# Gate and up of an expert pair issued expert by expert, with per-slot loads, an earlier lower-half scatter for the last pair and later LayerNorm parameter loads

## What is computed

```python
def moe(x, router_w, router_bias, w_gate, w_up, w_down, sw_gate, sw_up, sw_down):
    ...
    def expert_block(args):
        b_tok, b_w, e = args
        xb = xt[b_tok]
        h = jax.nn.silu(xb @ w_gate[e]) * (xb @ w_up[e])
        return (h @ w_down[e]) * b_w[:, None].astype(xt.dtype)
    ...
    routed = jax.ops.segment_sum(y_rows.reshape(rows, d), row_tok, num_segments=t)
    shared = (jax.nn.silu(xt @ sw_gate) * (xt @ sw_up)) @ sw_down
    return (routed + shared).reshape(bsz, s, d)
```

## Time and profile before

| | us |
|---|---|
| runs (three) | 1239.41, 1241.08, 1244.82; median 1241.08 |
| the profiled execution, its own time | 1241.98 |
| its span | 1240.2 |
| TensorE busy in it | 1183.7 (95%) |
| gate and up of both layers, L1216, busy | 226.8 + 118.6 + 115.3 |
| down projection, L1272 from `ew`, busy | 218.4 |

### The profile page before, as it was taken

One profiled execution on the slowest core, in us unless ns is written; L12 is line 12 of the kernel. 1 busy time (PEld: TensorE's weight loads), 2 busy tenths in 40 slices (PEclk: granted clock), 3 DMA queues, 4 the chain that ended last, 5 costly groups with the idle time before them and its releaser, 6 DMA issues.

```text
span 1240.2 us, 17629 instructions
## 1 busy us (share of the span) xinstructions
PE 1183.7 (95%) x7261; PEld 546.2 (44%) x7261; DVE 489.9 (40%) x1059; ACT 193.6 (16%) x330; POOL 47.2 (4%) x78
## 2 busy tenths in 40 slices
PE   9999999999999999988899999999999999998886
PEld 8774833333333333332386757333333333333322
DVE  5895733332323332322237157333333232332224
ACT  3231311111111111110122313111111111111102
POOL 6300100000000000000010001000000000000000
PEclk9999999999999999999989999999999999999998
DMA  9788799999999999999953596999999999999995
GB/s 348 211 300 360 297 383 412 414 422 420 421 421 422 421 421 421 421 421 420 402 190 126 202 382 248 392 414 407 421 421 420 420 422 420 422 421 421 420 420 215
DMA packets 83642, 463.98 MB, mean 374 GB/s; under 512 B 9264, under 2 KB 10608, under 8 KB 38384
## 3 DMA queue, kind: packets, MB, share of 16 engines
q1 hardware_dynamic: 83424, 462.37, 92.2%
q10 hardware_dynamic: 144, 0.52, 0.1%
HBM read 456.51 MB, written 6.36 MB: 373 GB/s over the span
## 4 chain that ended last, share of the span: by engine, by line
PE 72%; DMA 22%; DVE 2%; SPq 1%; ACT 1%; issue 1%; DVEq 0%; POOL 0%; POOLq 0%
PE bank L1216 30%; DMA expert_weights<-in_exp_w_up 21%; PE bank L1272 12%; PE bank L724 5%; PE bank L738 4%; PE bank L1136 4%; PE bank L1166 3%; PE bank L812 2%; PE bank L1154 2%; DMA weight_ring<-in_sh_w_up 1%; PE bank L839 1%; PE bank L1085 1%; PE bank L828 1%; PE bank L1159 1%; PE bank L1232 1%; SPq L316 1%
## 5 line engine op out<-in xcount | busy, mean ns | idle before, releaser
L1216 PE MATMUL bank<-expert_weights,weight_ring 128*64 128x512 f32 x1024 | 226.8, 595 | 12.3 <-DMA expert_weights<-in_exp_w_up 12.3
L1272 PE MATMUL bank<-expert_weights,hiddenT 128*32 128x512 f32 x1888 | 218.4, 595 | 7.8 <-DVE hiddenT L2097 3.6
L2094 DVE TENSOR_TENSOR hidden<-silu_gate,bank 128x256 f32<-128x256 f32 x64 | 26.9, 421 | 391.7 <-ACT silu_gate L1492 391.7
L1216 PEld LDWEIGHTS bank<-expert_weights,weight_ring 128*64 128x64 f32 x1024 | 70.6, 137 | 166.6 <-issue 139.7
L1216 PE MATMUL bank<-expert_weights,hT 128*64 128x512 f32 x512 | 118.6, 606 | 17.2 <-DMA expert_weights<-in_exp_w_up 17.2
L1272 PEld LDWEIGHTS bank<-expert_weights,hiddenT 128*32 128x32 f32 x1888 | 56.4, 109 | 159.3 <-issue 138.9
L1216 PE MATMUL bank<-expert_weights,octet_high 128*64 128x512 f32 x512 | 115.3, 592 | 0.0
L2106 DVE TENSOR_SCALAR y_top<-bank,slot_gate 128x512 fp32r<-128x512 f32 x64 | 48.0, 750 | 126.2 <-PE bank L1272 126.2
L1492 ACT ACTIVATE silu_gate<-bank 128x256 f32<-128x256 f32 x64 | 24.7, 386 | 438.4 <-PE bank L1216 438.4
L1496 ACT ACTIVATE y_top<-bank,slot_gate 128x512 fp32r<-128x512 f32 x64 | 44.0, 687 | 286.4 <-PE bank L1272 286.4
L1216 PEld LDWEIGHTS bank<-expert_weights,hT 128*64 128x64 f32 x512 | 34.3, 138 | 101.4 <-issue 64.5
(11 more groups left out here) (388 smaller groups left out, 1114.2 us busy)
## 6 DMA issues: line engine op xcount, KB each, us to landing
expert_weights<-in_exp_w_down SPq DMA_DIRECT2D x114, 1024.0 KB, 17.2
expert_weights<-in_exp_w_gate SPq DMA_DIRECT2D x108, 1024.0 KB, 14.2
expert_weights<-in_exp_w_up SPq DMA_DIRECT2D x108, 1024.0 KB, 16.3
expert_weights<-in_exp_w_gate SPq DMA_DIRECT2D x40, 512.0 KB, 9.1
expert_weights<-in_exp_w_up SPq DMA_DIRECT2D x40, 512.0 KB, 10.9
weight_ring<-in_w_in_even SPq DMA_DIRECT2D x5, 2048.0 KB, 11.6
spare_down<-in_exp_w_down SPq DMA_DIRECT2D x10, 1024.0 KB, 11.8
weight_ring<-in_w_out SPq DMA_DIRECT2D x4, 2048.0 KB, 7.8
```

The lines of the kernel that those rows point to most:

```text
L1216: last_mm = nc.tensor.matmul(bank[6][a * 2 * CAP:(a + 1) * 2 * CAP, :].rearrange("p (w f) -> p w f", w=2), octet_tokens(l, v, c)[:, 2 * q ...
L1272: last_mm = nc.tensor.matmul(bank[b][by_tile:by_tile + CAP, :], hm[:, j, own:own + CAP], down[a][:, j, half * 512:(half + 1) * 512], start ...
L2094: nc.vector.tensor_tensor(hslot[:, :], sg[:, :], bank[6][:, DE:2 * DE], ALU.mult)\
```

## The change

1. Gate and up of a pair are issued expert by expert: the loop over `a` is now outside the loop over the chunks `c`. TensorE waits for each expert's loads by itself (`gu_in` has one semaphore per slot), and the end of the first expert increments a new semaphore, `gu_first`.
2. SP reloads the first expert's slot after `gu_first` and the second's after `gu_full`. The loads by chunk halves (`expert_chunks`, `BY_HALVES`, `gu_part`, `second_part`, `last_part`) are gone; every gate and up load is of 1 MB.
3. `scatter_last` waits for the lower half's parts (`y_lo`, which `y_low` of columns 0 to 511 now increments too) and adds the lower column half of both tiles, then waits for `y_parts` and adds the upper half.
4. SP waits for the last pair's `gu_full` before it loads LayerNorm's parameters.

```diff
@@ -204,11 +204,9 @@
                   "bt ct stored c_in b_in direct gla_ln gla_last decays masked hstat hstd yhead states y_s5 "
                   "gelu5 out_full")
         for l in range(2):
-            for name in ("gu_in", "d_in"):
-                MO[l][name] = [sem(f"moe{l}_{name}{u}") for u in range(2)]
-            MO[l]["second_part"] = sem(f"moe{l}_second_part")
-            MO[l]["last_part"] = sem(f"moe{l}_last_part")
-            MO[l]["gu_part"] = sem(f"moe{l}_gu_part")
+            MO[l]["gu_in"] = [sem(f"moe{l}_gu_in{s}") for s in range(NSLOT)]
+            MO[l]["d_in"] = [sem(f"moe{l}_d_in{u}") for u in range(2)]
+            MO[l]["gu_first"] = sem(f"moe{l}_gu_first")
             MO[l]["spare_in"] = sem(f"moe{l}_spare_in")
         ring_in = [sem(f"ring_in{i}") for i in range(2)]
 
@@ -313,16 +311,8 @@
         def expert_load(sp, m, l, e, s):
             src_g = A["exp_w_gate"][l, e].rearrange("(p c) f -> p (c f)", c=KC)
             src_u = A["exp_w_up"][l, e].rearrange("(p c) f -> p (c f)", c=KC)
-            sp.dma_start(ew[:, s, 0:EW], src_g).then_inc(m["gu_in"][s // 2], 16)
-            sp.dma_start(ew[:, s, EW:2 * EW], src_u).then_inc(m["gu_in"][s // 2], 16)
-
-        def expert_chunks(sp, l, e, s, chunks, landed):
-
-            lo, hi = chunks[0] * DE, (chunks[-1] + 1) * DE
-            src_g = A["exp_w_gate"][l, e].rearrange("(p c) f -> p (c f)", c=KC)
-            src_u = A["exp_w_up"][l, e].rearrange("(p c) f -> p (c f)", c=KC)
-            sp.dma_start(ew[:, s, lo:hi], src_g[:, lo:hi]).then_inc(landed, 16)
-            sp.dma_start(ew[:, s, EW + lo:EW + hi], src_u[:, lo:hi]).then_inc(landed, 16)
+            sp.dma_start(ew[:, s, 0:EW], src_g).then_inc(m["gu_in"][s], 16)
+            sp.dma_start(ew[:, s, EW:2 * EW], src_u).then_inc(m["gu_in"][s], 16)
 
         def down_half(sp, l, e, s, part, landed):
 
@@ -410,7 +400,6 @@
         def spare_load(sp, m, a, src):
             sp.dma_start(spare_d[a][:, :, :].rearrange("p j n -> p (j n)"), src).then_inc(m["spare_in"], 16)
 
-        BY_HALVES = (2, 3, 4, 5)
         LATE_SLOTS = ((2, 3), (3,))
         LN_INPUT = {"mix0": M0["out_full"], "mix1": M1["out_full"], "moe0": MO[0]["acc_full"], "moe1": MO[1]["acc_full"]}
         LAST_PARTS = ((0, 0, D), (1, 0, 512), (1, 512, D))
@@ -437,57 +426,53 @@
             spare_load(sp, m, 1, down_src(l, 5))
             sp.dma_start(ew[:, 3, 2 * EW:3 * EW], down_src(l, 7)).then_inc(m["d_in"][1], 16)
 
-            def refill(base, it, u, down=None):
-
-                sp.wait_ge(m["gu_full"], (base - 1) * 2 + u + 1)
-                for s in (2 * u, 2 * u + 1):
+            def refill_gu(base, it, u):
+
+                for s, read in ((2 * u, "gu_first"), (2 * u + 1, "gu_full")):
+                    sp.wait_ge(m[read], (base - 1) * 2 + u + 1)
                     expert_load(sp, m, l, it * NSLOT + s, s)
+
+            def refill_d(base, u, experts):
+
                 sp.wait_ge(m["y_hi_full"], (base - 1) * 2 + u + 1)
-                for s in (2 * u, 2 * u + 1):
-                    e = down[s - 2 * u] if down else it * NSLOT + s
+                for s, e in experts:
                     sp.dma_start(ew[:, s, 2 * EW:3 * EW], down_src(l, e)).then_inc(m["d_in"][u], 16)
 
-            def early_refill(ps, pair):
-
-                u = pair % 2
-                first = 2 * pair - 2 * u
-                later = m["last_part" if u else "second_part"]
-                if pair in BY_HALVES:
-                    sp.wait_ge(m["gu_part"], len(BY_HALVES) * ps + BY_HALVES.index(pair) + 1)
-                    for s in (2 * u, 2 * u + 1):
-                        expert_chunks(sp, l, first + s, s, range(0, 4), m["gu_in"][u])
-                sp.wait_ge(m["gu_full"], ps * PAIRS + pair - 1)
-                for s in (2 * u, 2 * u + 1):
-                    if pair in BY_HALVES:
-                        expert_chunks(sp, l, first + s, s, range(4, KC), later)
-                    else:
-                        expert_load(sp, m, l, first + s, s)
-                if pair == 6:
-                    return
-                sp.wait_ge(m["y_hi_full"], ps * PAIRS + pair - 1)
-                if pair == 4:
-                    for a in range(2):
-                        spare_load(sp, m, a, down_src(l, 12 + a))
-                    return
-                for s in (2,) if pair == 3 else (2 * u, 2 * u + 1):
-                    e = first + s + (NSLOT if pair == 2 else 0)
-                    sp.dma_start(ew[:, s, 2 * EW:3 * EW], down_src(l, e)).then_inc(m["d_in"][u], 16)
+            def refill(base, it, u):
+
+                refill_gu(base, it, u)
+                refill_d(base, u, [(s, it * NSLOT + s) for s in (2 * u, 2 * u + 1)])
+
+            def early_refills(ps):
+
+                base = ps * (NE // NSLOT) + 1
+                refill_gu(base, 1, 0)
+                refill_d(base, 0, ((0, 8), (1, 9)))
+                refill_gu(base, 1, 1)
+                refill_d(base, 1, ((2, 6),))
+                base = ps * (NE // NSLOT) + 2
+                refill_gu(base, 2, 0)
+                sp.wait_ge(m["y_hi_full"], (base - 1) * 2 + 1)
+                for a in range(2):
+                    spare_load(sp, m, a, down_src(l, 12 + a))
+                refill_gu(base, 2, 1)
+                refill_d(base, 1, ((2, 10), (3, 11)))
+                base = ps * (NE // NSLOT) + 3
+                refill_gu(base, 3, 0)
+                refill(base, 3, 1)
 
             def last_refill(ps):
 
-                sp.wait_ge(m["gu_full"], ps * PAIRS + PAIRS - 2)
-                for chunks, landed in ((range(0, 4), m["gu_in"][1]), (range(4, KC), m["last_part"])):
-                    for s in (2, 3):
-                        expert_chunks(sp, l, NE - NSLOT + s, s, chunks, landed)
-                sp.wait_ge(m["y_hi_full"], ps * PAIRS + PAIRS - 2)
+                base = ps * (NE // NSLOT) + NE // NSLOT - 1
+                refill_gu(base, NE // NSLOT - 1, 1)
+                sp.wait_ge(m["y_hi_full"], (base - 1) * 2 + 2)
                 for part, landed in enumerate((m["d_in"][1], m["spare_in"])):
                     for s in (2, 3):
                         down_half(sp, l, NE - NSLOT + s, s, part, landed)
 
             def refills(ps):
 
-                for pair in range(2, OCT):
-                    early_refill(ps, pair)
+                early_refills(ps)
                 with sp.Fori(OCT // 2, NE // NSLOT - 1) as it:
                     for u in range(2):
                         refill(ps * (NE // NSLOT) + it, it, u)
@@ -500,11 +485,13 @@
             with sp.If(npass > 1):
                 with sp.Fori(1, npass) as ps:
                     refill(ps * (NE // NSLOT), 0, 0)
-                    refill(ps * (NE // NSLOT), 0, 1, down=(2, 7))
+                    refill_gu(ps * (NE // NSLOT), 0, 1)
+                    refill_d(ps * (NE // NSLOT), 1, ((2, 2), (3, 7)))
                     spare_load(sp, m, 2, down_src(l, 3))
                     for a in range(2):
                         spare_load(sp, m, a, down_src(l, 4 + a))
                     refills(ps)
+            sp.wait_ge(m["gu_full"], npass * PAIRS)
             sp_ln_params(sp, k, A["ln2_w"][l], A["ln2_b"][l])
             return npass
 
@@ -1139,14 +1126,19 @@
 
             def scatter_last(par):
 
+                def add(t, n):
+                    for part in (y_top, y_low):
+                        last = nc.tensor.matmul(bank[2 * t + n][:, :], onehotT[slot_rows(t), par, :],
+                                                part[slot_rows(t), n * 512:(n + 1) * 512], start=False,
+                                                stop=(part is y_low), skip_group_check=True)
+                    return last
+
+                pe.wait_ge(m["y_lo"], npass * (2 * PAIRS))
+                add(0, 0).then_inc(m["acc_full"], 1)
+                add(1, 0)
                 pe.wait_ge(m["y_parts"], npass * PAIRS + 1)
-                for t in range(TT):
-                    for n in range(2):
-                        for part in (y_top, y_low):
-                            last = nc.tensor.matmul(bank[2 * t + n][:, :], onehotT[slot_rows(t), par, :],
-                                                    part[slot_rows(t), n * 512:(n + 1) * 512], start=False,
-                                                    stop=(part is y_low), skip_group_check=True)
-                        last.then_inc(m["acc_full"], 1)
+                add(0, 1).then_inc(m["acc_full"], 1)
+                add(1, 1).then_inc(m["acc_full"], 2)
 
             def add_alpha_h(t, n, part):
 
@@ -1203,22 +1195,17 @@
                         elif q == 0:
                             pe.wait_ge(m["xg_lo"], n + 4)
                             pe.wait_ge(m["xg_hi"], n + 4)
-                        pe.wait_ge(m["gu_in"][u], 64 * g + 64)
-                        for c in range(KC):
-                            if opening:
```

(20 more changed lines are left out.)

## The result

The changed kernel takes 1545.35 us (median of four runs, 1544.11 to 1546.6) against 1240.61 us for the kernel before on the same chips: a ratio of 1.2445, with a 95% interval of 1.2424 to 1.2465. It is 304.7 us slower. The forecast was 1537 us, within 1508 to 1566.

The account below looks back on a forecast made before the run. It took DMA and TensorE as nearly balanced, DMA slightly ahead. From the profiled 1241.98 us, + 330.2 (order) - 33.2 (DMA waits) - 1.3 (scatter) gave 1537.7, less 0.9 to the median: 1537 us, range 1508 to 1566.

Parts of the forecast that it names:

- The bound and its flip: In the MoE pairs: DMA slightly ahead at 14.9 us becomes TensorE the bound at 18.6 us a pair.
- Twelve slots a pair: Gate and up: 28 record times of 0.43 us instead of 16, 5.16 us more per pair, 330.2 us in all.
- rows 8: Profile of scatter_last before: four records on each row half start two by two within 0.81 us, cited for three waiting records.
- Full overlap: Gate and up: other case, where the expert order makes the kernel not slower; chance 4%.
- a slower clock: TensorE's clock: other case, where it falls instead of staying at 1.00; chance 2%.
- The 33.2 us of DMA waits that go: TensorE's 23 waits on expert weights vanish: 29.5 us idle plus 23 x 0.16 us, 33.2 us less.
- Loads by slot cost nothing here: Expert loads in the MoEs: dropping the early halves costs nothing while TensorE is 3.7 us a pair slower than loads.
- The scatter: End of each MoE: LayerNorm's first statistics start earlier, 0.65 us less per layer, 1.3 us in all.
- LayerNorm's parameters: Loads issued on SP after the last gate and up: no cost taken, bounds 0 and 4 us.
- That is covered, and the rest is due later: Loads for mix1 behind LayerNorm's parameters: issued 9.3 us ahead of their first reader, 2.5 MB needing 6.2 us, cost 0.

Follow-up runs that it names:

- The single-change run: The kernel before with only the order of gate and up changed to expert by expert, loads, waits and MoE end kept: 1541.23 us, ratio 1.2403.
- the runs with blocks of 8 and 16: The changed kernel with the two experts alternating every 8 matmul records: 1332.46 us; with 16 it is the changed kernel itself, 1545.35 us.
- the run without the halves: The changed kernel with the old alternation of experts at every chunk and without SP's wait for gu_full: 1245.09 us, ratio 1.0021.

## Why the prediction was right, point by point

**The bound and its flip: right.** Both halves were measured: the old one nearly balanced, 13.4 us of TensorE's work in a plain pair against 14.9 us of loads, the new one TensorE's alone, 18.6 us, without a single DMA wait on expert weights.

**Twelve slots a pair: right in mechanism and number.** The second expert starts 5.20 us in, and gate and up takes 12.22 us, as written. The price was 5.16 us a pair, measured 12.22 - 7.02 = 5.20, over 64 pairs 2.6 us more than the term. The single-change run puts the whole of it on the order. One argument for it was weaker than written: rows 8, with groups of four, show that at 512 columns the other half starts past three waiting records, but not that it stops there. That three is the limit at 512 columns too, the runs with blocks of 8 and 16 showed, where the other half started 1.77 and 5.20 us in. That records on the same columns take a full slot each stood in the 5.16 us as the author's estimate. No row of the kernel before shows it for half of the array at 512 columns; the changed kernel does, with one record in flight at 523.75 and twelve slots in 5.20 us. Full overlap, gate and up at 7 us, did not come, and neither did a slower clock: it was 1.00 in the windows of both MoE stages.

**The 33.2 us of DMA waits that go: right within 2 us.** From the first start of gate and up to that of the last one in a layer, the changed kernel takes 592.1 us in both layers, the kernel before 448.6 and 446.0. 31 pairs at 5.20 are 161.2 us, so what went is 17.7 and 15.1 us, 32.8 in all. Not all of it is waits. In moe0 of the kernel before the granted clock fell to 0.50 once, from 590.1 to 593.5, behind a wait of 1.96 us for expert weights, and that pair's gate and up took 8.71 us instead of 7.02:

```profile
589.47 5.35 PE L1216 MATMUL bank<-expert_weights,hT 128*64 128x512 f32 x16 [1.96 <-DMA expert_weights<-in_exp_w_up]
```

```profile
590.10:593.50 3.40, 3.40 (x12) 0.98 (x8) 0.00 (x0) 0.00 (x0) 0.00 (x0) 0.50 1.01 407
```

That is 1.7 us of clock, and 31.1 us of waits, 2 us less than forecast. That the two sums meet within 0.4 us is in part luck.

**Loads by slot cost nothing here: right, but for the wrong pairs.** The text put the danger, were the cover gone, at the 8 early pairs, up to 3.5 us each. With the cover gone they cost nothing, and the last pair of each layer did, about 2 us each. The step mis-sized is the one that lumped `last_refill` with `BY_HALVES` as feeding a saturated queue. The DMA engines are as busy at a layer's end (share 1.03 to 1.07, 398 to 419 GB/s, from 600 to 612 us in the run without the halves). But no further gate and up stands behind the last pair's, and what counts then may be how soon its first chunks are there. That reading is argued; the runs show the cost and where it falls.

**The scatter: right,** 0.6 us an end in the profile for the 0.65 taken.

**LayerNorm's parameters: this is the step that failed,** and with the 2.6 us above it makes most of the 8 us by which 1545.35 lies above 1537. "That is covered, and the rest is due later", taken 0 with a bound of 4 us, measured 4.8 us in the changed kernel and about 6 us in the kernel before, above its bound in both. The parameters themselves were in time. The count stopped at the first load that mix1 reads. That one was issued 9.6 us ahead of its reader, against 9.3 forecast, and was in time. Behind it stand the ring's 2 MB, another 1.5 MB and six small loads, and the first and the last of these are what TensorE waited for. No term had the clock either: it stayed at 0.50 for 13.7 us, where it was 3.4 us in the run without SP's wait. The two waits make 3.4 of the 4.8 us, so the rest may be the clock's.

## What to carry to other kernels

Two small matmuls on different halves of TensorE's array overlapped here only where they were near each other in the program, with at most three earlier records waiting. Alternate the halves at least every four records (two float32 matmuls), which took 7.07 us here, where blocks of 8 took 8.90; a loop order that looks free made gate and up take 12.2 us instead of 7.0. A wait on a queue has to be priced by everything queued behind it up to the next stage's last early reader (4.8 us in the changed kernel), not by the load that it guards. And the load split in halves paid at a stage's last pair (about 4 us in all), not in the early pairs.

## What the runs showed of the hardware

TensorE started matmuls out of program order where they were on different halves of the array: with blocks of 4, 8 and 16 records the other half started at once, beside the fifth and beside the thirteenth (0, 1.77 and 5.20 us after the first; with blocks of 4 two records are in flight in the first 0.10 us), always with three earlier records still waiting by the count of slots. The runs with blocks of 4 and 8 records took 7.07 and 8.90 us, where strict order, counted in slots of 0.43 us, would need 10.8 and 12.5. Whether the reach is counted in matmuls or in instructions with their weight loads is open: every record here has its own weight load (7261 of each in the changed kernel), and it was not tried otherwise.

With half of the array's columns idle in 24 of 28 slots of each gate and up, the granted clock stayed at 1.00 through both MoE stages of the changed kernel, up to their last matmuls (windows from 160 to 768 us and from 948 to 1537.3). It fell to 0.50 in TensorE's wait for LayerNorm ahead of mix1 (at 769.4 us) and again behind moe1's last matmuls (at 1537.4).
